# The first block's projections: all high-half matmuls of a weight piece, then all its low-half matmuls, with a wait ahead of each

## What is computed

```python
h = rms_norm(x, a_norm[layer])
q, k, v, g = jnp.split(h @ a_w_in[layer], 4, axis=-1)      # 2048 x 16384
...
x = x + (o * jax.nn.silu(g)) @ a_w_out[layer]              # 4096 x 2048
...
k_s, v_s = jnp.split(h_kv @ kv_w, 2, axis=-1)              # 2048 x 8192
q, g = jnp.split(h @ b_w_in[lb], 2, axis=-1)               # 2048 x 8192
...
x = x + (o * jax.nn.silu(g)) @ b_w_out[lb]                 # 4096 x 2048
```

## Time and profile before

| | |
|---|---|
| median of 3 runs | 2673.71 us |
| lowest and highest | 2672.54 and 2674.64 us |
| the profiled execution, its time | 2672.86 us |
| its span | 2671.1 us |
| TensorE (PE) busy | 2643.2 us, 99% |
| VectorE (DVE) busy | 1830.6 us, 69% |
| ScalarE (ACT) busy | 1354.2 us, 51% |
| mean busy share of the DMA engines in each slice | 30 to 70% |

### The profile page before, as it was taken

One profiled execution on the slowest core, in us unless ns is written; L12 is line 12 of the kernel. 1 busy time (PEld: TensorE's weight loads), 2 busy tenths in 40 slices (PEclk: granted clock), 3 DMA queues, 4 the chain that ended last, 5 costly groups with the idle time before them and its releaser, 6 DMA issues.

```text
span 2671.1 us, 45331 instructions
## 1 busy us (share of the span) xinstructions
PE 2643.2 (99%) x16733; PEld 2373.5 (89%) x16733; DVE 1830.6 (69%) x2740; ACT 1354.2 (51%) x2060; POOL 132.2 (5%) x141
## 2 busy tenths in 40 slices
PE   8999999999999999999999999999999999999998
PEld 7888888888888888888888888888999899999887
DVE  7656566665675576666666666755889996689976
ACT  6444444444454454444444444544574674465664
POOL 0000000000000001101010010000000000000000
PEclk9999999999999999999999999999999999999999
DMA  7667666666666656667676666665555665566663
GB/s 229 211 192 212 194 198 203 191 211 196 200 197 189 188 163 204 198 197 204 191 211 195 201 200 192 199 195 189 180 168 180 185 189 170 166 192 185 207 212 126
DMA packets 513658, 514.76 MB, mean 193 GB/s; under 512 B 26922, under 2 KB 502466, under 8 KB 513282
## 3 DMA queue, kind: packets, MB, share of 16 engines
q1 hardware_dynamic: 490260, 488.01, 59.9%
q10 hardware_dynamic: 23296, 25.36, 3.2%
HBM read 489.93 MB, written 21.53 MB: 191 GB/s over the span
## 4 chain that ended last, share of the span: by engine, by line
PE 83%; DVE 10%; ACT 3%; issue 2%; DMA 1%; ACTq 0%; SPq 0%; DVEq 0%
PE proj L1346 34%; PE proj L1349 17%; PE proj L1361 9%; PE proj L1365 4%; PE proj L1531 4%; PE proj L1532 4%; PE proj L1533 4%; DVE scratch L2327 2%; DVE w_both L2168 2%; PE proj L1725 2%; PE ps_s L1436 1%; PE ps_s L1422 1%; PE proj L1727 1%; DMA scratch<-probabilities 1%; ACT w_both L963 1%
## 5 line engine op out<-in xcount | busy, mean ns | idle before, releaser
L1346 PE MATMUL proj<-operand,w_both 128*128 128x512 f32 x3968 | 1255.4, 398 | 1.8 <-issue 1.3
L1824 DVE TENSOR_TENSOR w_both<-w_raw,w_both 128x1024 fp32r<-128x1024 f32 x644 | 794.8, 1237 | 654.8 <-ACT w_both L738 654.0
L738 ACT ACTIVATE w_both<-w_raw 128x1024 fp32r<-128x1024 f32 x644 | 678.0, 1058 | 861.8 <-PE proj L1349 643.2
L1349 PEld LDWEIGHTS proj<-operand,w_both 128*128 128x128 f32 x3968 | 745.4, 188 | 176.1
L1349 PE MATMUL proj<-operand,w_both 128*128 128x256 f32 x3968 | 779.8, 278 | 0.0
L1346 PEld LDWEIGHTS proj<-operand,w_both 128*128 128x128 f32 x3968 | 606.9, 189 | 4.3 <-issue 1.7
L1531 PE MATMUL proj<-operand,w_both 128*128 128x272 f32 (+2 forms) x1540 | 447.1, 290 | 5.2 <-DVE w_both L2168 5.0
L1532 PE MATMUL proj<-operand,w_both 128*128 128x272 f32 (+2 forms) x1540 | 442.3, 287 | 0.0
L1533 PE MATMUL proj<-operand,w_both 128*128 128x272 f32 (+2 forms) x1540 | 442.0, 287 | 0.0
L2168 DVE TENSOR_TENSOR w_both<-w_raw,w_both 128x1024 fp32r<-128x1024 f32 x226 | 274.3, 1219 | 112.8 <-ACT w_both L963 112.0
L1361 PE MATMUL proj<-w_both,operand 128*128 128x512 f32 x1024 | 321.7, 395 | 0.0
(11 more groups left out here) (365 smaller groups left out, 2074.3 us busy)
## 6 DMA issues: line engine op xcount, KB each, us to landing
w_raw<-in_a_w_in_dram SPq DMA_DIRECT2D x256, 512.0 KB, 3.7
w_raw<-in_w_in_dram SPq DMA_DIRECT2D x160, 512.0 KB, 3.8
w_raw<-in_b_w_in_dram SPq DMA_DIRECT2D x128, 512.0 KB, 3.9
w_raw<-in_kv_w_dram SPq DMA_DIRECT2D x128, 512.0 KB, 4.2
w_raw<-in_a_w_out_dram SPq DMA_DIRECT2D x64, 512.0 KB, 4.5
w_raw<-in_b_w_out_dram SPq DMA_DIRECT2D x64, 512.0 KB, 4.4
w_raw<-in_w_out_dram SPq DMA_DIRECT2D x64, 512.0 KB, 3.5
probabilities<-scratch ACTq DMA_DIRECT2D x32, 384.0 KB, 2.5
```

What stands on the lines that cost most here:

```text
L738: act.activation(w_hi[:, s], w_raw[:, s], ACT.Copy).then_inc(hi_ready, 1)
L1346: pe.matmul(proj[:, 2 * bank + t, :], w_hi[:, s, kk, t * P:(t + 1) * P], rhs[:, k, :], start=first and k == 0, stop=False)
L1349: m = pe.matmul(proj[:, 2 * bank + t, 0:S], w_lo[:, s, kk, t * P:(t + 1) * P], rhs[:, k, 0:S], start=False, stop=last and end)
L1824: dve.tensor_tensor(w_lo[:, s], w_raw[:, s], w_hi[:, s].bitcast(F32), ALU.subtract).then_inc(pieces_split, 1)
```

## The change

Only `multiply` is changed. The four row tiles of a piece are gone through twice. The first time, behind a wait for `hi_ready` alone, come the eight matmuls with `w_hi` (16 when `summed`); the second time, behind the wait for `pieces_split`, the eight with `w_lo`. The matmuls, their operands, their banks and the count of `pieces_used` are the same as before.

```diff
                 for s in range(PIECES):
-                    pe.wait_ge(pieces_split, unit * PIECES + s + 1 + PIECES)
+                    ks = range(s * PK, (s + 1) * PK)
+                    pe.wait_ge(hi_ready, unit * PIECES + s + 1)
                     if chunk_wait is not None:
                         chunk_wait(s)
-                    for kk in range(PK):
-                        k = s * PK + kk
-                        end = k == KT - 1
-                        if summed:
-                            for t in range(2):
-                                cols = slice(t * P, (t + 1) * P)
+                    for kk, k in enumerate(ks):
+                        for t in range(2):
+                            weights = w_hi[:, s, kk, t * P:(t + 1) * P]
+                            start = first and k == 0
+                            if summed:
                                 out = proj[:, 2 * bank + t, 0:S]
-                                pe.matmul(out, w_hi[:, s, kk, cols], rhs[:, k, 0:S], start=first and k == 0, stop=False)
-                                pe.matmul(out, w_hi[:, s, kk, cols], rhs[:, k, S:512], start=False, stop=False)
-                                m = pe.matmul(out, w_lo[:, s, kk, cols], rhs[:, k, 0:S], start=False, stop=last and end)
-                        else:
-                            for t in range(2):
-                                pe.matmul(proj[:, 2 * bank + t, :], w_hi[:, s, kk, t * P:(t + 1) * P], rhs[:, k, :],
-                                          start=first and k == 0, stop=False)
-                            for t in range(2):
-                                m = pe.matmul(proj[:, 2 * bank + t, 0:S], w_lo[:, s, kk, t * P:(t + 1) * P], rhs[:, k, 0:S],
-                                              start=False, stop=last and end)
+                                pe.matmul(out, weights, rhs[:, k, 0:S], start=start, stop=False)
+                                pe.matmul(out, weights, rhs[:, k, S:512], start=False, stop=False)
+                            else:
+                                pe.matmul(proj[:, 2 * bank + t, :], weights, rhs[:, k, :], start=start, stop=False)
+                    pe.wait_ge(pieces_split, unit * PIECES + s + 1 + PIECES)
+                    for kk, k in enumerate(ks):
+                        for t in range(2):
+                            m = pe.matmul(proj[:, 2 * bank + t, 0:S], w_lo[:, s, kk, t * P:(t + 1) * P], rhs[:, k, 0:S],
+                                          start=False, stop=last and k == KT - 1)
                     m.then_inc(pieces_used, 1)
```

## The result

| | before | after |
|---|---|---|
| median of 22 runs each | 2673.72 us | 2677.51 us |
| lowest and highest | 2671.63 to 2675.72 | 2675.27 to 2680.6 |
| profiled execution, its span | 2671.1 us | 2676.0 us |
| PE busy | 2643.2 us | 2649.9 us |

The changed kernel is slower: the ratio is 1.0013, with a 95% interval of 1.0007 to 1.0019. That is 3.8 us, where 1.0 us less was forecast. The time lies in the forecast range and on this side of 0.2%, but the sign is wrong.

What follows compares the result with a forecast made beforehand. TensorE's own matmul rate was taken as the bound. From the 2673.71 us median, -1.0 us for the start and 0 each for second wait and matmul order gave 2672.7 us, range 2664 to 2686.

Steps and rivals of the forecast that it cites:

- The bound: Whole kernel: TensorE's own matmul rate sets the time, busy for 2643.2 of 2671.1 us.
- The waits: Ahead of each piece's matmuls: a second, already fulfilled wait costs 0; at most 2.6 us for 512 waits.
- The start: First unit: TensorE begins about 1.3 us earlier; after later waits -1.0 us remains, bounds 0 and -1.8.
- The cap: Unit 2's last piece: its low half, ready at 46.79, comes no earlier, leaving 0.98 of 1.2 us won.
- The order of the matmuls: 496 pieces: costs add whatever the order, 0.2283 and 0.1199 us, so a piece stays 2.786 us; term 0.
- The mild loss: Rival, runs in each piece: 512s at 0.2300, 256s at 0.1199, 2.799 us a piece, +6.6 us, 2679.3 us; chance 0.18.
- Its source: Earlier trace's run of 512-column matmuls with weights of only 64 columns: 0.2300 us each over 12 distances.
- Fewer changes are a gain: Rival, size changes in a piece: one instead of four, 3.6 ns each, -5.4 us, 2667.3 us; chance 0.20.
- The strong loss: Rival, 256s in runs bound by weight load: 0.232 and 0.1199, 2.815 us a piece, +14.6 us, 2687.3 us; chance 0.10.
- the signs that were to show the forecast right: In the trace: PE busy within 3 us, low-half idle at most 1 us, first weight matmul about 13 us, piece 2.786 us.
- the 0.52 for no change: Chance that the whole kernel's time stays within about 0.2%, between 2668.4 and 2679.1 us.
- the unknown: Whole kernel: something not in the profile rows decides the time; chance 0.04.

Runs made afterwards that it cites:

- the fours: Kernel before with four matmuls of 512 columns then four of 256, twice a piece, one wait; 2680.83 us, ratio 1.0028.
- two waits in twos: Kernel before, its matmul order kept, with both waits: hi_ready ahead of the piece, pieces_split ahead of the first low-half matmul; 2674.43 us, ratio 1.0003.
- twos: Order of the kernel before: two matmuls of 512 columns, two of 256, four times a piece; 2673.72 us.
- one wait in eights: Changed kernel's order, eight 512s then eight 256s, with only the wait for pieces_split ahead of the piece; 2677.95 us, ratio 1.0017 against the kernel before.
- eights: Order of the changed kernel: eight matmuls of 512 columns, then eight of 256 in a piece; 2677.51 us with two waits.
- sixteens: Against the kernel before, two pieces taken together: sixteen matmuls of 512 columns, then sixteen of 256; 2673.27 us, ratio 0.9998.
- the mix of threes and a two: Kernel before with runs of three, three and two in each piece, 512s then 256s, one wait; 2678.37 us, ratio 1.0019.
- runs of one: Kernel before with 512 and 256 in turn: 256 on the same bank, 2690.93 us, ratio 1.0067; on the other column half, 2687.76 us, ratio 1.0054.

## Why the prediction was wrong

- **The bound** was read rightly: the time follows TensorE's pace. In every experiment the difference of the times is the difference of a piece's time in the output stage times 496, with the start where it changed, within 3 us. The largest miss is the fours, whose 7.5 us make 15 ns a piece over all pieces, where the output stage alone shows 20.
- **The waits** were right. The second wait costs nothing that shows (two waits in twos: ratio 1.0003 and the same 2.787 us a piece; one wait in eights: the loss remains). No idle time stands ahead of a matmul with the low half in the changed kernel.
- **The start** came out at 0.91 us for 0.98, but by luck: two steps of its working were wrong. Piece 3 was to begin at 22.5, when its operand is done, 1.2 us earlier. It began at 22.77, behind piece 2, which had itself waited for its operand until 19.90. So 0.95 us were won there, of which 0.91 are left at the first scores. The cap, the low half of unit 2's last piece, did not hold: that low half was said not to come earlier than 46.79. In the changed kernel it is done at 45.13, and TensorE takes it 1.7 us later, without idle time:

```profile
43.91 1.22 DVE L1823 TENSOR_TENSOR w_both<-w_raw,w_both 128x1024 fp32r<-128x1024 f32 x1
...
46.85 0.63 PE L1360 MATMUL proj<-w_both,operand 128*128 128x512 f32 x2
```

- **The order of the matmuls** is the step that failed: "if costs simply add, whatever the order". From the twos a 512 was worked out at 0.2283 us, which is a price inside twos alone. The settled price is 0.2266, and in runs of eight it measured 0.230. The term put at 0 is +3.3 us. The mild loss, 0.230 and 0.120 and 2.799 us a piece, had the direction and the paces; measured 0.230, 0.119 and 2.793. It was forecast at +6.6 us, twice the size. Its source, met the 0.230 by coincidence: in the trace the distances there are 228, 224, 227, 234, 230, 236, 229, 224, 227, 234, 230, 236 ns. The first three behind the 256s are not dear, and the dear ones come back every six to the end of the run, which the runs of eight and sixteen do not show.
- **Fewer changes are a gain** was wrong as a rule for eights: from 1 to 2 a change and back becomes cheaper, from 2 to 8 dearer (4 to 21 ns), so three changes fewer did not pay for the one that is left.
- **The strong loss** had the pace of the 256s right, 0.115 in twos and 0.120 in a long run; what failed is that the 512s would stay at 0.232, since from the sixth on they take 0.227. Whether the weight load sets the 0.120 was not tested. The 0.11 us of the earlier trace rows bounds a load from above only: those matmuls of the scores have a slower pace of their own, 0.218 us for 256 columns against 0.120 in the weight products.
- Of the signs that were to show the forecast right, two failed: PE busy is 6.7 us higher, outside the 3 us, and a piece takes 2.793 us and not 2.786. The chances do not add up as told either: a third of the mild loss is put on this side of the limit, but the 0.52 for no change holds only the forecast and the unknown.
- The 109 and 216 ns that the prediction works out from the Trainium skill, TensorE: Matmul & The Clock Gate, section "Back-to-back issue gap", are there the gap of a single matmul taken by itself, and not of a stream with weight loads. The 228 ns set beside them are the solved price of a 512 in twos; the settled pace measured 226.6. No term of the sum hung on either.
- The first block's 3968 + 3968 matmuls made the sum sensitive: an error of 7 ns in 2.79 us a piece turned the sign.

## What to carry to other kernels

When a kernel is bound by TensorE and its matmuls follow each other without gaps, a reordering is not free even if the same matmuls remain: work out the settled pace of each size from long runs, and look at what is above it around each change of size, in each pattern that the trace has. A pace solved from one pattern holds in that pattern only. A mean from another pattern may meet the right number for another reason, as the earlier trace rows did; look at the single distances in it before taking it. And split a wait only where it is late: here in one unit of 128, which gives the start's gain without the reordering in the others.

## What the runs showed of the hardware that was not expected

- The distance between matmuls of 128x128 weights depends on the sizes of those that came before: a 512 takes 0.2266 us in a long run of its kind, 0.230 in the mean of eight and 0.232 in fours; a 256 takes 0.1199 us in a long run and 0.1186 in the mean of fours. In the eights and sixteens a 512 has its settled pace from the sixth behind a change on.
- The price of a change of size and back depends on the run length: 7, 4, 17, 21 and 23 ns for 1, 2, 4, 8 and 16, and 8 in the mix of threes and a two. It did not change with the bank in runs of one, two and eight, with another operand tile and its weights in twos, or with the reversed order in eights. In the second block's pairs, where weights and operand change places, it is 3.5 ns for runs of one; why is open.
- A wait on TensorE that is fulfilled when it comes is not visible in the pace, not even a second one in each 2.8 us (2.787 us a piece in twos with one wait and with two, 2.793 in eights).
